# Query-key products of an encoder layer: three single passes of rounded operands and their remainders, in place of plain f32

## What is computed

```python
q = partial_rope(rms_norm(q.reshape(B, S, heads, width), q_norm))
k = partial_rope(rms_norm(k.reshape(B, S, heads, width), k_norm))
# 8 "B" heads: two parts of 64 columns each, p = softmax(scale * q_c . k_c) for c = 0, 1
a = p[:, :, 0] - lam * p[:, :, 1]
out = a @ v
# 8 "A" heads: one part of 128 columns, softmax over three dilated windows, as one mask added to the scores
```

## Time and profile before

| | |
|---|---|
| median of 3 runs | 1810.29 us (1810.03 to 1811.79) |
| the profiled execution | 1812.05 us, its span 1810.2 us |
| PE busy | 1799.7 us (99%) |
| PEld busy | 1493.1 us (82%) |
| DVE busy | 1551.0 us (86%) |
| ACT busy | 1071.3 us (59%) |
| chain that ended last | PE 98%, DVE 1% |
| DMA | 351.95 MB, mean 194 GB/s |

### The profile page before, as it was taken

The page is one execution under the profiler, slowest core; times in us unless marked ns, Lnnn a source line. Parts: engine busy times, 40 slices in busy tenths (PEclk is TensorE's granted clock), DMA queues, the critical chain, the costliest instruction groups (busy, mean ns, idle before and its releaser), DMA issues.

```text
span 1810.2 us, 22774 instructions
## 1 busy us (share of the span) xinstructions
PE 1799.7 (99%) x8225; PEld 1493.1 (82%) x8225; DVE 1551.0 (86%) x1612; ACT 1071.3 (59%) x1294; POOL 43.6 (2%) x73
## 2 busy tenths in 40 slices
PE   8999999999999999999999999999999999999999
PEld 7788888888888888888888888888888888888887
DVE  5899999999999888667666666799999999998986
ACT  5666666566656565556556655566666666666553
POOL 0000000000000000111010000000000000000000
PEclk9999999999999999999999999999999999999999
DMA  7655555555356556654555455755555555354654
GB/s 267 256 206 217 217 195 212 206 185 186 117 186 218 211 199 220 204 178 148 168 165 180 162 163 181 261 186 204 190 205 216 217 196 211 108 191 164 234 205 143
DMA packets 178390, 351.95 MB, mean 194 GB/s; under 512 B 7168, under 2 KB 8208, under 8 KB 178064
## 3 DMA queue, kind: packets, MB, share of 16 engines
q1 hardware_dynamic: 178288, 351.02, 55.1%
q10 hardware_dynamic: 32, 0.01, 0.0%
HBM read 348.91 MB, written 2.10 MB: 194 GB/s over the span
## 4 chain that ended last, share of the span: by engine, by line
PE 98%; DVE 1%; ACT 0%; DMA 0%; issue 0%; SPq 0%; ACTq 0%
PE acc L523 13%; PE acc L524 13%; PE acc L525 13%; PE acc L585 8%; PE acc L583 8%; PE acc L584 8%; PE turn L597 4%; PE turn L596 4%; PE turn L598 4%; PE acc L596 3%; PE acc L597 3%; PE acc L598 3%; PE turn L554 1%; PE turn L663 1%; PE turn L662 1%; PE turn L664 1%
## 5 line engine op out<-in xcount | busy, mean ns | idle before, releaser
L1258 DVE TENSOR_TENSOR w_lo<-w_raw,w_hi 128x1024 fp32r<-128x1024 f32 x168 | 206.1, 1238 | 141.1 <-ACT w_hi L894 131.3
L894 ACT ACTIVATE w_hi<-w_raw 128x1024 fp32r<-128x1024 f32 x167 | 176.2, 1060 | 195.2 <-PE acc L525 178.0
L911 ACT ACTIVATE w_hi<-b 128x1024 fp32r<-128x1024 f32 x200 | 212.6, 1063 | 119.0 <-PE acc L585 77.4
L925 ACT ACTIVATE w_hi<-w_raw 128x1024 fp32r<-128x1024 f32 x176 | 185.6, 1059 | 120.1 <-PE acc L525 88.3
L585 PE MATMUL acc<-w_hi,h_lo 128*128 128x512 f32 x640 | 249.0, 389 | 0.0
L583 PE MATMUL acc<-w_hi,h_hi 128*128 128x512 f32 x640 | 249.0, 389 | 0.0
L584 PE MATMUL acc<-w_lo,h_hi 128*128 128x512 f32 x640 | 249.0, 389 | 0.0
L1279 DVE TENSOR_TENSOR w_lo<-w_raw,w_hi 128x1024 fp32r<-128x1024 f32 x176 | 212.8, 1222 | 31.8 <-ACT w_hi L925 28.5
L1269 DVE TENSOR_TENSOR w_lo<-b,w_hi 128x1024 fp32r<-128x1024 f32 x200 | 236.5, 1219 | 0.0
L911 ACT ACTIVATE w_hi<-w_raw 128x1024 fp32r<-128x1024 f32 x160 | 169.6, 1061 | 91.8 <-PE acc L585 64.2
L523 PE MATMUL acc<-w_hi,h_hi 128*128 128x512 f32 x512 | 204.1, 399 | 5.6 <-DVE h_lo L1296 4.4
(11 more groups left out here) (208 smaller groups left out, 3258.4 us busy)
## 6 DMA issues: line engine op xcount, KB each, us to landing
w_raw<-in_ffn_w_in SPq DMA_DIRECT2D x95, 1024.0 KB, 4.9
w_raw<-in_ffn_w_out SPq DMA_DIRECT2D x88, 1024.0 KB, 5.1
b<-in_ffn_w_in SPq DMA_DIRECT2D x80, 1024.0 KB, 4.9
w_raw<-in_w_in SPq DMA_DIRECT2D x48, 1024.0 KB, 5.0
w_raw<-in_w_out SPq DMA_DIRECT2D x16, 1024.0 KB, 5.0
x_sb<-in_x SPq DMA_DIRECT2D x3, 512.0 KB, 10.8
out_y<-x_sb SPq DMA_DIRECT2D x3, 512.0 KB, 8.9
w_raw<-in_ffn_w_in SPq DMA_DIRECT2D x2, 512.0 KB, 6.9
```

The source lines that it names most:

```text
L894: nc.scalar.activation(w_hi[:, u % RING, 0:count, :], w_raw[:, slot, k0:k0 + count, :], ACT.Copy).then_inc(hi_ready, 1)
L911: nc.scalar.activation(w_hi[:, slot, :, :], in_raw(piece)[:, k0:k0 + UK, :], ACT.Copy).then_inc(hi_ready, 1)
L925: nc.scalar.activation(w_hi[:, u % RING, :, :], src, ACT.Copy).then_inc(hi_ready, 1)
L1258: nc.vector.tensor_tensor(w_lo[:, slot, 0:count, :], w_raw[:, v // 2 % RAW, k0:k0 + count, :], w_hi[:, slot, 0:count, :].bitcast(F32), ALU ...
```

## The change

ACT writes the turned queries and keys as f32r (`qk_hi`, the function is now `round_qk`). A new function on DVE, `split_qk`, writes what is left of them into `qk_lo`: per head two operations of 128x256 that read PSUM, the gain column and `qk_hi`. It stands in DVE's `attention_step` in phase 0, ahead of the units of that step. Each product of `scores` is now three matmuls of f32r in place of one of f32 (which the trace shows as two records with a weight load each). For a B head all products of part 0 come first, then all of part 1, as before. `scores` and `values` wait for `qk_split`, which DVE counts up, in place of `qk_t_ready` of ACT.

```diff
-            qk_t = sb("qk_t", [P, 2, SEQ], F32, attention)
+            qk_hi = sb("qk_hi", [P, 2, SEQ], F32R, attention)
...
+            qk_lo = sb("qk_lo", [P, 2, SEQ], F32R, attention)
...
             def scores(u):
-                pe.wait_ge(qk_t_ready, u + 1)
+                pe.wait_ge(qk_split, u + 1)
...
                     for t in range(TT):
-                        mm = nc.tensor.matmul(score[:, c, t, :], qk_t[part, 0, t * P:(t + 1) * P],
-                                              qk_t[part, 1, :], start=True, stop=True)
+                        for n, (q, k) in enumerate(((qk_hi, qk_hi), (qk_hi, qk_lo), (qk_lo, qk_hi))):
+                            mm = nc.tensor.matmul(score[:, c, t, :], q[part, 0, t * P:(t + 1) * P], k[part, 1, :],
+                                                  start=n == 0, stop=n == 2)
...
                 if u + 1 < HEADS:
-                    pe.wait_ge(qk_t_ready, u + 2)
+                    pe.wait_ge(qk_split, u + 2)
...
-                    s = nc.scalar.activation(qk_t[:, a, :], qk_turn[:, a, :], ACT.Copy, scale=gain_col[:, n:n + 1])
-                s.then_inc(qk_t_ready, 1)
+                    s = nc.scalar.activation(qk_hi[:, a, :], qk_turn[:, a, :], ACT.Copy, scale=gain_col[:, n:n + 1])
+                s.then_inc(qk_hi_ready, 1)
...
+            def split_qk(u):
+
+                dve.wait_ge(qk_hi_ready, u + 1)
+                if u == 0:
+                    dve.wait_ge(col_ready, 3)
+                for a in range(2):
+                    n = a + (TT if u < B_HEADS else 0)
+                    s = nc.vector.scalar_tensor_tensor(qk_lo[:, a, :], qk_turn[:, a, :], gain_col[:, n:n + 1],
+                                                       qk_hi[:, a, :].bitcast(F32), ALU.mult, ALU.subtract)
+                s.then_inc(qk_split, 1)
...
             def attention_step(s):
 
                 u, phase = divmod(s, 3)
+                if phase == 0 and u < HEADS:
+                    split_qk(u)
                 if phase == 1 and u < HEADS:
                     maxima(u)
```

More of the change, by code:

```diff
@@ L319, in hybrid_layer_kernel @@
         qk_turned = sem("qk_turned")
-        qk_t_ready = sem("qk_t_ready")
+        qk_hi_ready = sem("qk_hi_ready")
+        qk_split = sem("qk_split")
         scored = sem("scored")
@@ L1116, in copy_chunk, with round_qk @@
                     nc.scalar.activation(squares[:, :, :], qkv[:, g % 2, kind, :, :], ACT.Square).then_inc(qk_squared, 1)
-            def copy_qk_t(u):
+            def round_qk(u):
                 act.wait_ge(qk_turned, u + 1)
@@ L1174, in attention_step @@
                     if u < HEADS:
-                        copy_qk_t(u)
+                        round_qk(u)
                     if 1 <= u <= HEADS:
```

## The result

The changed kernel takes 1837.19 us (median of 4 runs, 1834.96 to 1838.65), the kernel before beside it 1810.78 (1810.03 to 1811.79): a ratio of 1.0142, with an interval of 1.0129 to 1.0154, 26.4 us slower. The forecast had the sign right and 13.8 us, about half of the loss; 1837.2 lies above the range, which ended at 1831. The profiled execution has a span of 1836.4 us (1838.12 us in all), 26.2 us more than before.

What follows compares the result with a forecast made beforehand. PE was taken as the bound from end to end, without slack. Products -2.8 us and waits +16.6 us gave +13.8 us on the median of 1810.29 us: 1824.1 us, range 1820 to 1831.

Steps and rivals of the forecast that it cites:

- PE is the bound and nothing gives time back: Whole kernel: PE busy 1799.7 of 1810.2 us, without slack, so any microsecond it waits is lost.
- The wait, the term that decides: PE at `values` waits for DVE's `split_qk`, which stands behind earlier DVE work such as `scale_qk`: 16.6 us in all.
- DVE is there in time: Rival at PE's waits for DVE: waits vanish, leaving the products' gain, 1807.5 us; 6%, partial forms 5%.
- the clock falls: Rival in the attention steps: new idle times lower PE's granted clock, up to 17 us more, 1841; 3%.
- The products on PE: `scores` matmuls in sixteen heads: three f32r passes at 0.115 us each replace f32, -2.8 us (bounds -3.3 and -2.2).
- if the two parts still run side by side: Condition for B heads on PE: six pairs of matmuls, 0.69 us for 0.86, a gain of 0.17 a head.
- a rival of 14%: Products on PE: passes cost more than f32, by lost overlap in B heads (1829.7 us) or uncovered loads (1833.6); 14% together.
- The rival's second form: Products on PE: loads not covered by the matmul ahead on the same rows, +0.42 us in sixteen heads, 1833.6; little of 14%.
- The operations on DVE: Two new DVE operations per head take 0.88 us, 14 us in all; delaying `w_lo` by that costs nothing.

Runs made afterwards that it cites:

- the last two runs: The changed kernel with DVE's operations earlier, plus a B head's two parts taking turns one by one or product by product: 1809.19 and 1809.25 us.

## Why the prediction was wrong

**PE is the bound and nothing gives time back**: right. The waits, 16 us, are in the total in full.

**The wait, the term that decides**: right, in place and nearly in size. Foretold were 2.15 us at heads 2 and 3, 2.07 at 6, 7, 10 and 11, 3.1 at 13, 0.5 at 12, 16.6 in all; measured 2.15, 2.05 to 2.06, 2.83, 0.5, 16.0. That DVE comes late again in each head, since ACT and so PE's pace starts its long piece, held; "DVE is there in time" did not happen, but the run with the earlier operations shows that it turned on that one point.

**The rival "the clock falls"**: this is the step that failed. It was costed at up to 17 us and given 3%, "for more than that". The two rows at hand were an idle time of 1.67 us without a fall and one of 4.59 us with one; the new waits lay between, and no row excluded a fall. Between such ends the cost should have stood in the range, as other unknown prices did. It came to 9.6 us, by the distances in the profiled execution and by the run with PE kept busy alike. The other part of the miss is the products' 3 us, below. With half of the seven waits taken to bring 2.4 us each, the sum would have been some 8 us higher, and a range up to the 1841 that the prediction had worked out for all seven would have held the time. The Trainium skill, "TensorE: Matmul & The Clock Gate", section Part 1, says that PE's lower clock is the state after idle time and the higher one follows activity; the runs agree, and show that idle times of 2.05 us can do it in the middle of dense work.

**The products on PE**: the size was wrong, -2.8 us foretold, +0.2 measured. The price of a matmul was right: 0.71 us for an A head's six where 0.69 was worked out. What failed is "if the two parts still run side by side", weighed as all or nothing, with the loss of it as a rival of 14% and +0.52 us a head. It was half: in the changed kernel a B head takes 9 intervals of some 0.115 us, where full pairing takes 6. With the parts in turns the foretold gain appears: 0.90 us for 1.07. With four f32 records of one part ahead (plain f32), or with three or one f32r matmuls (the last two runs), the parts pair fully; with six they don't. The same page of the Trainium skill, section Part 3, The mechanism, gives PE a window of 64 entries in which it pulls loads ahead; if that were the reach, six ahead would have changed nothing, so the runs speak for a much shorter one: the seventh matmul in the program started only when the third did. The rival's second form (loads not covered on the same rows) is excluded: 0.12 us from start to start in an A head.

**The operations on DVE**: right. 0.87 us for a pair where 0.88 was worked out, and the delay of the units behind them shows nowhere.

## What to carry to other kernels

A semaphore that moves from one engine to another brings with it everything that stands ahead of the new signaller in that engine's order: look at what is in front of the new instruction, not at how long it takes. If TensorE is the bound, waits of 2 to 3 us may cost more than their length through the clock (here some 10 us beside 16 us of waits), and the time then varies from execution to execution; idle times of 1.5 us did not do it here. Where matmuls of 64 rows can run side by side on the two halves of the array, let the halves take turns in the program: every one or three f32r matmuls paired fully here, six did not; four and five were not tried.

## What was not expected of the hardware

- Useless matmuls ahead of a wait made the kernel 9.6 us faster (1837.19 to 1827.58 us), by keeping the clock up. Half as many did as well (1827.78).
- Falls of the clock are not the same in each execution: 1833.3 to 1841.5 us, at mean granted clocks of 0.997 to 0.991, for one program with waits of fixed length.
- Two parts of a head pair up on PE although the program has them one behind the other, but only over a short distance: 1.07 us with four f32 records of one part ahead, 1.24 with six f32r matmuls, 0.90 with three or one. A matmul of one part even starts ahead of earlier ones of the other: the seventh at 790.60 us, the fifth and sixth at 790.82 and 790.93.
